# Expert weights in 16 KB runs and 2 MB places, the embedding product stored in DRAM during the experts, and the last up products by column halves

## The reference

```python
def expert_choice_ffn(xn, w_router, w_gate, w_up, w_down):
    B, S, D = xn.shape
    cap = CAPACITY_FACTOR * S // N_EXPERTS
    aff = jax.nn.softmax(jnp.einsum('bsd,de->bse', xn, w_router).astype(jnp.float32), axis=-1)
    top_aff, top_idx = lax.top_k(jnp.swapaxes(aff, 1, 2), cap)
    bidx = jnp.arange(B)[:, None, None]
    xg = xn[bidx, top_idx]
    hid = jax.nn.silu(jnp.einsum('becd,edf->becf', xg, w_gate)) * jnp.einsum('becd,edf->becf', xg, w_up)
    y = jnp.einsum('becf,efd->becd', hid, w_down) * top_aff[..., None].astype(xn.dtype)
    return jnp.zeros((B, S, D), dtype=y.dtype).at[bidx, top_idx].add(y)
...
        h = h + expert_choice_ffn(rmsnorm(h, norm_ffn[l]), w_router[l],
                                  w_exp_gate[l], w_exp_up[l], w_exp_down[l])
        ple_gate = jax.nn.sigmoid(rmsnorm(h, norm_ple[l]) @ w_ple_gate[l])
        h = h + ple_gate * (p[l] @ w_ple[l])
    return rmsnorm(h, norm_final)
```

## Time and profile before

| | us |
|---|---|
| runs of the kernel before | 2082.97, 2084.06, 2089.34 |
| median | 2084.06 |
| the profiled execution | 2090.52 |
| its span, first to last instruction | 2088.5 |
| PE busy in the span | 2051.5 |
| DVE, ACT busy | 987.6, 546.9 |
| experts, first gate product to last down product | 1552.1 to 2014.5 |
| tail | 2014.5 to 2088.5 |

### The profile page before, as it was taken

The page is one execution under the profiler, slowest core; times in us unless marked ns, Lnnn a source line. Parts: engine busy times, 40 slices in busy tenths (PEclk is TensorE's granted clock), DMA queues, the critical chain, the costliest instruction groups (busy, mean ns, idle before and its releaser), DMA issues.

```text
span 2088.5 us, 23656 instructions
## 1 busy us (share of the span) xinstructions
PE 2051.5 (98%) x9752; PEld 1383.0 (66%) x9752; DVE 987.6 (47%) x1457; ACT 546.9 (26%) x1078; POOL 29.6 (1%) x16
## 2 busy tenths in 40 slices
PE   9999999999999999999999999999999999999998
PEld 5677565876888777786678888868754444333357
DVE  3776544556655454674566657644541101101145
ACT  4745352320001232203222435330140000000024
POOL 0121000000000000000000000000000000000000
PEclk9999999999999999999999999999999999999999
DMA  8311111322222120223221211312659999999961
GB/s 212 81 41 49 57 58 41 81 101 78 84 81 91 46 76 31 81 81 68 85 81 41 81 41 41 81 52 81 242 206 397 416 405 419 420 419 420 419 240 41
DMA packets 117978, 316.79 MB, mean 152 GB/s; under 512 B 38064, under 2 KB 46384, under 8 KB 93680
## 3 DMA queue, kind: packets, MB, share of 16 engines
q1 hardware_dynamic: 115520, 313.28, 40.4%
q10 hardware_dynamic: 2352, 2.00, 0.4%
HBM read 312.83 MB, written 2.10 MB: 151 GB/s over the span
## 4 chain that ended last, share of the span: by engine, by line
PE 89%; DVE 4%; ACT 4%; issue 2%; DMA 1%; DVEq 0%; SPq 0%; ACTq 0%
PE bank L459 37%; PE bank L473 17%; PE bank L3056 10%; PE bank L3106 5%; PE bank L2970 2%; PE bank L2992 2%; PE bank L1837 2%; PE bank L1429 1%; PE bank L1407 1%; PE bank L1457 1%; PE bank L2558 1%; DMA wide<-in_w_exp_gate 1%; PE bank L2548 1%; PE bank L2984 1%; PE bank L2976 1%
## 5 line engine op out<-in xcount | busy, mean ns | idle before, releaser
L459 PE MATMUL bank<-hT,ring 128*128 128x256 f32 x1168 | 267.7, 383 | 0.5 <-ACT av L608 0.5
L459 PEld LDWEIGHTS bank<-hT,ring 128*128 128x128 f32 x1168 | 221.0, 192 | 36.2 <-issue 6.0
L473 PE MATMUL bank<-hT,ring 128*128 128x512 f32 (+1 forms) x416 | 187.4, 602 | 5.0 <-DMA ring<-in_l_w_in 5.0
L459 PE MATMUL bank<-l_quarter,l_quarter 128*128 128x256 f32 x672 | 153.8, 381 | 0.5 <-DVE rqk L1665 0.5
L473 PEld LDWEIGHTS bank<-hT,ring 128*128 128x128 f32 (+1 forms) x416 | 76.9, 190 | 96.8 <-issue 90.7
L459 PEld LDWEIGHTS bank<-l_quarter,l_quarter 128*128 128x128 f32 x672 | 126.0, 190 | 20.4 <-issue 3.0
L3056 PE MATMUL bank<-wide,xg 128*64 128x512 f32 x488 | 124.8, 595 | 0.8 <-DMA wide<-in_w_exp_gate 0.8
L3056 PE MATMUL bank<-ring,xg 128*64 128x512 f32 x352 | 100.2, 595 | 1.3 <-DMA ring<-in_w_exp_gate 1.3
L3224 DVE TENSOR_TENSOR xT<-bank,xT 128x512 f32<-128x512 f32 x32 | 22.1, 692 | 157.4 <-PE bank L2970 157.3
L3056 PEld LDWEIGHTS bank<-wide,xg 128*64 128x64 f32 x488 | 38.7, 137 | 75.2 <-issue 75.2
L459 PE MATMUL bank<-ring,hT 128*128 128x256 f32 x384 | 86.7, 381 | 0.2 <-DVE gv_hi L743 0.2
(11 more groups left out here) (573 smaller groups left out, 3357.8 us busy)
## 6 DMA issues: line engine op xcount, KB each, us to landing
wide<-in_w_exp_down SPq DMA_DIRECT2D x38, 1024.0 KB, 13.5
ring<-in_l_w_in SPq DMA_DIRECT2D x18, 2048.0 KB, 7.8
wide<-in_w_exp_gate SPq DMA_DIRECT2D x34, 1024.0 KB, 10.6
wide<-in_w_exp_up SPq DMA_DIRECT2D x27, 1024.0 KB, 14.1
ring<-in_w_exp_up SPq DMA_DIRECT2D x25, 1024.0 KB, 10.4
ring<-in_w_exp_down SPq DMA_DIRECT2D x21, 1024.0 KB, 15.1
ring<-in_w_in SPq DMA_DIRECT2D x10, 2048.0 KB, 8.4
ring<-in_w_exp_gate SPq DMA_DIRECT2D x19, 1024.0 KB, 11.7
```

What stands on the lines that cost most here:

```text
L459: mm = pe.matmul(self.out(n)[:, half * 256:half * 256 + 256], *halves[half][k], start=i == 0 and not job["goes_on"], stop=False, skip_grou ...
L473: mm = pe.matmul(self.out(n), *mats[i], start=i == 0, stop=i == len(mats) - 1)
```

## The change

Weights of the experts:

- A unit is now half of one expert's weight: 512 rows, four neighbouring rows on each partition, 2 MB with runs of 16 KB. It is loaded whole by one DMA into a place of 2 MB, or as two blocks of 1 MB (8 KB of the same runs each) into single places. The order is: half, expert, quarter. A half of a product needs the units of both experts.
- Six places of 2 MB: tiles 8 to 15, 16 to 23, both ring buffers, the memory of `hT`, and tiles 0 to 7. The last two join during pair 1: tiles 0 to 7 when the embedding's weight and the single place in it are done with, `hT` when the embedding product is in DRAM. Single places are used in the first pairs and are dropped as their limits pass; the last is used in pair 2. From pair 3 on all blocks go to the six large places, 12 MB.
- The rows that belong to one k are now every fourth one; `hid` and `rows_tm` are written in that order.

The embedding product: ACT, after each of its eight copies into `pw`, waits for the copy and issues a DMA of 256 KB to a DRAM tensor `embedded`. Behind all weights, after the last matmul that reads the large place `hT`, SP loads the eight pieces back into `pw`. The first `add_embedding` waits for all of them.

The up product: its second half goes through four k for column half 0 and then through four k for column half 1, and DVE's first `hid` instruction waits for column half 0 alone.

```diff
-                for q in range(4):
+                for half in range(2):
                     for e in range(2):
-                        stream.append((a[w][0, 2 * p + e, q * 256:(q + 1) * 256, :].rearrange("(p k) n -> p k n", k=2), 2, D))
-                        blocks.append(len(stream) - 1)
+                        four = a[w][0, 2 * p + e, half * 512:(half + 1) * 512, :].rearrange("(p k) n -> p k n", k=4)
+                        for q in range(2):
+                            stream.append((four[:, 2 * q:2 * q + 2, :], 2, D))
+                            blocks.append(len(stream) - 1)
+                            four_rows[len(stream) - 1] = four
...
+        fours = {n: four_at(x) for n, x in (
+            (1, at("wide_a", 8, [P, 4, D])[:, :, :]), (3, at("wide_b", 16, [P, 4, D])[:, :, :]),
+            (5, ring[WO2[0] % RING][:, 0:4 * D].rearrange("p (k n) -> p k n", k=4)),
+            (7, ring[WO2[1] % RING][:, 0:4 * D].rearrange("p (k n) -> p k n", k=4)),
+            (6, hT[:, :, :].rearrange("p (k c) n -> p k (c n)", c=2)),
+            (13, at("wide_c", 0, [P, 4, D])[:, :, :]))}
...
+        LIMIT = {LATER: NB + 8, 9: NB + 2, 10: NB, 11: 3 * NB, 12: NB, 15: 1, 16: 16}
+        FIRST = [(15, TOPMOST), (1,), (3,), (5,), (LATER, 9), (7,), (10, 11), (12, 16)]
...
+        for u in range(NB * len(EXP) // 2):
+            e = 2 * u
+            if u < len(FIRST):
+                places = [(n, None) for n in FIRST[u]]
+            else:
+                while waiting[0][0] in singles and (single_after(e + 1, 0) != 0 or single_after(e + 1, 1) is None):
+                    waiting.pop(0)
+                places = [waiting.pop(0)]
+                if places[0][0] in singles:
+                    places.append(waiting.pop(single_after(e + 1, 0)))
...
                     if j == WPG[1]:
-                        sp.wait_ge(tiles_done, max(last_tile[last_place[n]] for n in (EMB, 0)))
+                        sp.wait_ge(tiles_done, last_tile[last_of[EMB]])
...
+                elif by == "kept":
+                    sp.wait_ge(embedding_kept, 16 + 16 * KD)
                 elif by == "embedding":
                     sp.wait_ge(*place_free[by])
+                    sp.wait_ge(tiles_done, last_tile[last_of[LATER]])
...
-                last_tile[EXP[p][i]] = t0 + 24 * p + i + 1
+                last_tile[EXP[p][i]] = t0 + 24 * p + i // 4 * 4 + i % 2 * 2 + i // 2 % 2 + 1
...
         def even_first(x):
-            return x.rearrange("p (q r f) -> p q f r", q=2, r=2)
+            return x.rearrange("p (r f) -> p f r", r=4)
...
                 issue_blocks(sp, len(stream))
+                sp.wait_ge(tiles_done, last_tile[last_of[LENT]])
+                sp.wait_ge(embedding_kept, 16 + 16 * KD)
+                for m in range(KD):
+                    sp.dma_start(pw[m], embedded[m]).then_inc(embedding_back, 16)
...
-                            for k in range(4 * half, 4 * half + 4):
-                                pair = EXP[p][8 * which + k // 2 * 2:8 * which + k // 2 * 2 + 2]
-                                if k % 2 == 0:
+                            apart = which == 1 and half == 1
+                            ks = range(4 * half, 4 * half + 4)
+                            for k, ns in [(k, (n,)) for n in range(2) for k in ks] if apart else [(k, range(2)) for k in ks]:
+                                pair = [EXP[p][8 * which + 4 * half + 2 * e + k // 2 % 2] for e in range(2)]
+                                if k % 2 == 0 and 0 in ns:
                                     for j in pair:
                                         wait_block(pe, j)
-                                for n in range(2):
+                                for n in ns:
...
+                                if apart and ns == (0,) and k == KD - 1:
+                                    mm.then_inc(up_half, 1)
...
                     act.activation(pw[m], b, ACT.Copy).then_inc(pw_out, 1)
+                    act.wait_ge(pw_out, m + 1)
+                    act.dma_start(embedded[m], pw[m]).then_inc(embedding_kept, 16)
...
-                        dve.wait_ge(tiles_done, base + 16)
+                        if n == 0:
+                            dve.wait_ge(up_half, up_before + p + 1)
+                        else:
+                            dve.wait_ge(tiles_done, base + 16)
...
+            if i == 0:
+                dve.wait_ge(embedding_back, 16 + 16 * KD)
```

More of the change, by code:

```diff
@@ new lines, in build @@
+        early = [rows(at(f"wide{i}", 4 * i, [P, 2, D])) for i in range(2)]
+        fours = {n: four_at(x) for n, x in (
[4 more added lines that the diff above has]
+            (13, at("wide_c", 0, [P, 4, D])[:, :, :]))}
@@ L313, in build @@
+        level_of = {n: 16 if n < 5 or n >= TOPMOST else 32 if n < 9 else 96 if n == 9 else 64 for n in (*fours, *singles)}
         order = list(range(E0))
-        TOPMOST = 14
-        waiting = [(n, None) for n in (15, TOPMOST, *range(EMB), 16)]
-        for e in range(NB * len(EXP)):
-            n, by = waiting.pop(0)
-            while e >= LIMIT.get(n, e + 1):
-                n, by = waiting.pop(0)
-            j = E0 + e
-            order.append(j)
-            wide_at[j] = places[n]
-            taken_from[j] = by if by in (None, "embedding") else E0 + by
-            waiting.append((n, e))
-            if e == EMB_TO:
+        waiting = []
```

86 lines of the change are left out of this document (54 added, 32 removed).

## The result

| | before | changed |
|---|---|---|
| median of 20 runs each, taken in turns (us) | 2086.87 | 2089.76 |
| lowest, highest | 2082.32, 2090.15 | 2085.53, 2093.07 |
| ratio, 95% interval | | 1.0015 [1.0009, 1.0021] |
| profiled execution, its span | 2090.52, 2088.5 | 2086.19, 2084.0 |
| experts: first gate product to end of last down product | 1552.09 to 2014.51: 462.42 | 1546.02 to 2010.07: 464.05 |

A forecast was written before the change was run, and what follows sets the result against it. The prediction took the expert loads to bound the kernel, with PE's limit within about 2 us. A later experts' end, +4.5 us, and zeros for the other terms gave 2084.06 + 4.5 = 2088.6 us, range 2078 to 2095.5.

The forecast's parts named there:

- loads bound: Experts: weight loads rather than PE set the end; 2086 to 2091 us, chance 0.40.
- PE's work: Up-to-down handover, pairs 2 to 6: the down product begins 0.9 us earlier in each, 4.3 us off PE's path.
- Where the loads start: Pair 0: the second reuse of a place waits for the up product, so its block lands 10.4 us later, about 1574.4.
- How fast they run: Expert loads: 16 KB runs make a 2 MB unit 4.94 us, saving 0.05 us or 1.1%; last gate block lands 1968.4.
- The line through 2 KB and 8 KB packets: Packet cost from the WPG and expert loads: 7 ns a packet plus 76 ns for each 2 KB, so 16 KB takes 617 ns.
- The 3 us kept for delays: Expert loads: of 6.4 us lost to empty queues and single-engine delays, half was kept, 3 us.
- What PE then waits for: Pairs 5 to 7: PE waits about 11 us for loads against 2.2; experts end at 2019.0, +4.5 us.
- The whole-unit waits: Pair 7's gate product: the last wait moves to in front of k 4, 3.5 us more work behind it.
- The lent memory doesn't help: Experts: 12 MB of places against 11 bring nothing, since places aren't short where DMA is continuously busy.
- The embedding's way: Embedding to DRAM and back: ACT's issues 0.81 us each, cost 0, at most 0.6; ten microseconds of cover at read-back.
- Writes in fours: hid and rows_tm writes alternating among four rows, not two: taken as 0, bounds -0.9 to +1.8 us.
- faster loads outside the profile: Support for the faster, PE-bound rival (2077.6 us, chance 0.12): unprofiled executions, median 6.5 us lower, may load faster.

The follow-up runs named there:

- e2: The kernel before plus only the column halves of the up product: experts 462.28 us against 462.42, ratio to before 1.0005.
- e3: The changed kernel without the column halves of the up product: experts 464.02 us against 464.05, ratio to before 1.0020.
- e9: e8 without the column halves of the up product: experts 462.02 us against 457.89, ratio to before 1.0006.
- e8: The changed kernel with hT and wide_c opened for loads before the experts, an eighth of the embedding product moved ahead: experts 457.89 us against 464.05, ratio to before 0.9995.
- e1: The changed kernel with the first two reused places free earlier, so the second reuse isn't late: experts 463.74 us against 464.05, ratio to before 1.0012.
- e4: The changed kernel with each 2 MB unit loaded by two DMAs in 8 KB runs: experts 470.45 us against 464.05, ratio to before 1.0056.
- e7: The changed kernel without the embedding's DRAM round trip, hT not lent (five large places): experts 469.09 us against 464.05, ratio to before 1.0046.
- e13: The changed kernel with hT not lent, no round trip, and 8 KB runs by two DMAs a unit: experts 469.88 us, ratio to before 1.0038.
- e10: e4 with a semaphore for each half of a unit, so PE waits for half units: experts 467.86 us against 470.45, ratio to before 1.0034.
- e14: The changed kernel profiled again, unchanged: experts 463.91 us against 464.05, ratio to before 1.0014.
- e11: e8 with pair 7's four gate units each loaded by two DMAs with separate waits: experts 458.05 us against 457.89, ratio to before 0.9993.
- e12: e8 without the round trip and the lent hT, wide_c still opened early: experts 477.71 us against 457.89, ratio to before 1.0090.

## Why the prediction was right, and which of its steps were not

Forecast 2088.6, +0.2%, within 2078.0 to 2095.5; measured 2089.76, +0.15%. The case was the likeliest one, loads bound, and the waits show it. That the numbers agree so well is in part luck: of the forecast +4.5 us the experts show only 1.6, and 1.5 us of the measured 3.1 lie elsewhere, where I had forecast nothing; and the base of the sum, a median of 3 runs, lay 2.8 us under the median of 20. Step by step:

- **PE's work**: right. 0.90 us off each of five handovers, worth nothing while the loads run back to back (e2, e3), and 4.1 of the 4.5 us once they wait for places that PE frees (e9 against e8).
- **Where the loads start**: right as an event, wrong as a price. The second reuse landed at 1563.36 + 5.0, 22.3 us behind the first gate product, as predicted, and 10 us later than before. But e1 takes the delay away and gains 0.3 us. What I had not asked is what the loads would do with an earlier start: 16 MB of places stood full. This is the step of the prediction that failed, together with the lent memory below. The sum still came out, because behind the late start nothing else ran empty, so that counting units from there was sound. As a cause of the difference to before it isn't: the 10.4 us of delay are worth 0.3 (e1).
- **How fast they run**: right in kind, too small in size. A unit takes 4.90 us, not 4.94; the last gate unit of pair 7 landed 1959.70 - 1546.02 = 413.7 us behind the first product, not 416.3. 74 x 0.035 = 2.6 us is nearly all of the miss in the experts (1.6 us longer, where I had 4.5). This is the term that was mis-sized. The line through 2 KB and 8 KB packets gave 7 ns a packet; e4 against the changed kernel gives 0.085 us for 8 packets fewer on each engine, 11 ns each. The 3 us kept for delays were right: 413.7 - 22.3 = 391.4 us are 395 less 6.3 for the units plus 2.7. By the page "DMA: Bandwidth & Descriptors" of the Trainium skill, section "Why small descriptors are slow", the estimate was 0.03 us a unit. e4 measures nearly three times that, against the rule.
- **What PE then waits for**: 50.4 us from that landing to the end, 50.6 predicted. The waits come to 6.8, not 11: the loads were 2.6 us earlier, and 1.5 us went into products at half the clock, a term that the prediction didn't have. The whole-unit waits cost 2.6 of the 3.5 us (measured with 8 KB runs). "The lent memory doesn't help" is **wrong**: 5.0 us (e7). I argued that places aren't short where the DMA is continuously busy. It was busy because of them.
- **The embedding's way**: cost 0, right; ACT's issues took 0.33 to 0.35 us each, not 0.81, between copies that wait for PE anyway (ACT's timeline):

```profile
1532.30 0.60 ACT L3171 ACTIVATE hT<-bank 128x512 f32<-128x512 f32 x1 [1.12 <-PE bank L3015]
1532.92 0.33 ACTq L3173 DMA_DIRECT2D embedded<-hT  x1
```

  The read-back was issued at 2010.57, and its issues to landing are 8.5 us in the middle, 7.7 for the second `WPG`; DVE's first use at 2033.47 still waited for ACT and not for them, as in the earlier trace rows:

```profile
2033.47 0.42 DVE L3377 TENSOR_TENSOR ple_gate<-ple_gate,hT 128x256 f32<-128x256 f32 x1 [0.55 <-ACT ple_gate L3424]
```

- **Writes in fours**: 0, right. Groups of DVE (1550 to 2015) and ACT (1515 to 1560) against the earlier trace rows, which had 1063 and 1141 ns:

```profile
L3324 DVE TENSOR_TENSOR hid<-bank,pos 128x512 f32<-128x512 f32 x16 | 17.0, 1062 | 100.2 <-PE bank L3097 100.2
L3194 ACT ACTIVATE rows_tm<-bank,ffn_rc 128x512 f32<-128x512 f32 x8 | 7.5, 1118 | 0.0
```

  By the cacheline note of the Trainium skill ("SBUF — State Buffer", section "Door 1: the DMA port swizzle") both patterns pay at every element. The trace agrees: both cost the same, and more than the 692 ns of a plain write.

So what does the change do? Its parts, in the experts: what is left of it without the longer runs and the lent memory, so five places of 2 MB instead of eleven of 1 MB, whole-unit waits, the late start and the column halves, costs 469.88 - 462.42 = 7.5 us (e13). No run parts these 7.5 us further; that the whole-unit waits are 2.6 of them is measured with six places (e10), and that the column halves add nothing is carried over from e3. Longer runs and the lent memory together give 5.8 back. 1.6 us is the rest.

**Still open.** The whole program is 3.1 us slower by the ratio (1.9 to 4.4), the experts explain 1.5 to 1.6. The other 1.5 us are placed only in part. The two profiled executions with the same clock ahead of the experts, the kernel before (2090.52) and e14 (2092.83), differ by 2.3 us: 1.5 in the experts, 0.2 ahead of them, 0.5 in the tail and 0.1 outside the span. Of these the tail's is no more than scatter, since tails of 74.0 and 74.7 us both occur with the code of before (in e2 the latter), and 73.9 to 74.8 with that of the changed kernel. The granted clock ahead of the experts also bears on the 6.5 us by which the profiled execution of before lay above its median. The prediction had thought of faster loads outside the profile, but whole times go with the clock: among the 27 runs of the kernel before that stand beside e1, those with a mean clock of 0.999 took 2082.9 us on average and those with 0.995 took 2087.3.

## To carry to other kernels

When two resources are both full, ask of each gain not only "is it on the path" but "which limit comes next". The end of such a stage can be set by when the loads start, by their rate, by the places that the consumer frees, or by the consumer's own work, and a gain in one is worth what the next leaves of it (0.8 and -0.6 us alone, 5.8 together). A continuously busy DMA is no proof that memory is ample; count what the queue would do with one place fewer. And a late start of a queue costs nothing if full places would have stopped it anyway.

## What the hardware did that I hadn't expected

- PE's clock after a wait. Behind the 2.71 us wait in pair 6 the granted clock was 0.50 (1.2 of 2.4 GHz) from 1940 to 1942 and the products took 1.06 to 1.12 us instead of 0.59; it was back at 1.00 by 1944. Behind waits of 1.28 us and less it stayed at 1.00. But a long wait isn't always followed by it: e3's wait of 2.78 us, e7's second one of 2.85, e11's of 2.43 and both of e13's of 2.89 left the clock at 1.00, while waits of 2.71 to 2.97 us in this and seven other runs, the first one of e7, and a wait of 9.95 us in e12 were followed by 0.50. What decides stays open. PE's timeline and the table by stretch of the changed kernel:

```profile
1940.21 1.08 PE L3149 MATMUL bank<-wide_c,hidT 128*64 128x512 f32 x1 [2.71 <-DMA hT<-in_w_exp_down]
1941.09 1.06 PE L3149 MATMUL bank<-wide_c,hidT 128*64 128x512 f32 x1
```

```profile
1940.00:1942.00 2.00, 1.79 (x6) 0.64 (x8) 0.00 (x0) 0.00 (x0) 0.00 (x0) 0.50 1.04 442
```

  The next wait for a load hides the loss, some 1.5 us. e4 and e13 both wait 2.89 us for the same load of pair 6; in e4 the clock falls and the next wait is 1.31 us, in e13 it stays and the next wait is 2.89:

```profile
1958.53 0.61 PE L3101 MATMUL bank<-wide_a,xg 128*64 128x512 f32 x1 [1.31 <-DMA wide_b<-in_w_exp_gate]
1958.58 0.61 PE L3095 MATMUL bank<-wide_b,xg 128*64 128x512 f32 x1 [2.89 <-DMA ring<-in_w_exp_gate]
```

  In e8 no wait for a load follows, and the loss is in its 457.89.

- The issue of a 256 KB DMA from ACT costs 0.33 us where its runs are 2 KB, against 0.81 for one of 16 KB with runs of 64 bytes.
- Doubling a packet from 8 to 16 KB, where I had expected 1.1%, moved 420 to 427 GB/s: 1.7%.
